# Expert slabs of a mixture-of-experts stage loaded as two transfers of 64 partitions instead of one of 128

## The reference

```python
def _moe(h, router, wg, wu, wd):
    logits = jnp.einsum('btd,de->bte', h, router).astype(jnp.float32)
    top_v, top_i = lax.top_k(logits, TOP_K)
    probs = jax.nn.softmax(top_v, axis=-1)
    ...
    for e in range(N_EXPERTS):
        y = y + combine[..., e:e + 1].astype(h.dtype) * _swiglu(h, wg[e], wu[e], wd[e])
```

## Time and profile before

| | us |
|---|---|
| Median of 3 runs (lowest to highest) | 1567.94 (1566.75 to 1570.85) |
| Profiled execution, its own time | 1572.46 |
| Its span (first to last instruction) | 1570.6 |
| PE busy in the span | 1526.9 (97%) |
| DVE, ACT, POOL busy | 631.3, 321.6, 56.3 |
| Queue 1 (SP's), share of 16 DMA engines over the span | 47.4% |

### The profile page before, as it was taken

The page is one execution under the profiler, slowest core; times in us unless marked ns, Lnnn a source line. Parts: engine busy times, 40 slices in busy tenths (PEclk is TensorE's granted clock), DMA queues, the critical chain, the costliest instruction groups (busy, mean ns, idle before and its releaser), DMA issues.

```text
span 1570.6 us, 39489 instructions
## 1 busy us (share of the span) xinstructions
PE 1526.9 (97%) x17595; PEld 1254.2 (80%) x17595; DVE 631.3 (40%) x1456; ACT 321.6 (20%) x759; POOL 56.3 (4%) x68
## 2 busy tenths in 40 slices
PE   9999999999999999999999999999999999999976
PEld 6877776887779999987887777877778797788765
DVE  5133346744145656562234267542241221122213
ACT  1432113222112222133321222221120000000001
POOL 1000010110000000000000000200010000000000
PEclk9999999999999999999999999999999999999998
DMA  8333435213544444346425252116779988989992
GB/s 338 108 107 115 168 116 138 88 30 85 207 143 159 142 155 161 108 169 249 155 101 207 93 137 94 44 64 210 309 297 340 335 304 332 342 297 335 354 401 98
DMA packets 64324, 299.71 MB, mean 191 GB/s; under 512 B 21839, under 2 KB 23567, under 8 KB 37663
## 3 DMA queue, kind: packets, MB, share of 16 engines
q1 hardware_dynamic: 50392, 268.10, 47.4%
q0 software_dynamic: 2944, 18.09, 3.1%
q10 hardware_dynamic: 10823, 11.05, 2.7%
HBM read 277.93 MB, written 19.28 MB: 189 GB/s over the span
## 4 chain that ended last, share of the span: by engine, by line
PE 93%; DVE 3%; issue 2%; DMA 1%; ACT 1%; SPq 0%; DVEq 0%; ACTq 0%
PE ps L1007 15%; PE ps L1593 15%; PE ps L1743 14%; PE ps L1468 11%; PE ps L1675 7%; PE ps L1475 6%; PE ps L1531 4%; PE ps L994 4%; PE ps L1324 2%; PE ps L1626 2%; DMA ring<-in_mix 1%; PE ps L1019 1%; PE ps L1300 1%; PE ps L1057 1%; PE ps L1372 0%
## 5 line engine op out<-in xcount | busy, mean ns | idle before, releaser
L1007 PE MATMUL ps<-xn,ring 128*128 128x288 f32 x928 | 238.1, 413 | 0.0
L1007 PEld LDWEIGHTS ps<-xn,ring 128*128 128x128 f32 x928 | 174.9, 192 | 50.8 <-issue 2.8
L1468 PE MATMUL ps<-xn,ring 128*128 128x288 f32 x768 | 203.0, 412 | 0.8 <-ACT gate L2074 0.4
L1468 PEld LDWEIGHTS ps<-xn,ring 128*128 128x128 f32 x768 | 142.1, 190 | 48.9 <-issue 11.7
L1593 PE MATMUL ps<-y_ml,arena 128*64 128x96 f32 (+5 forms) x3584 | 142.7, 242 | 17.1 <-issue 16.2
L1593 PEld LDWEIGHTS ps<-y_ml,arena 128*64 128x64 f32 x3584 | 139.1, 140 | 22.4 <-issue 22.3
L1743 PE MATMUL ps<-arena 128*128 128x144 f32 x1028 | 133.4, 285 | 0.9 <-DVE arena L2911 0.9
L1743 PEld LDWEIGHTS ps<-arena 128*128 128x128 f32 x1028 | 129.3, 189 | 1.0 <-issue 1.0
L1675 PE MATMUL ps<-arena,mixed 128*32 128x256 f32 x2024 | 112.2, 379 | 2.6 <-issue 2.6
L1675 PEld LDWEIGHTS ps<-arena,mixed 128*32 128x32 f32 x2024 | 65.9, 110 | 45.8 <-issue 4.0
L2859 DVE TENSOR_TENSOR mixed<-ps,mixed 128x96 f32<-128x96 f32 (+5 forms) x88 | 21.7, 247 | 193.8 <-PE ps L1593 193.6
(11 more groups left out here) (514 smaller groups left out, 1849.0 us busy)
## 6 DMA issues: line engine op xcount, KB each, us to landing
arena<-in_egu SPq DMA_DIRECT2D x56, 1024.0 KB, 6.0
ring<-in_mix SPq DMA_DIRECT2D x46, 1024.0 KB, 6.1
arena<-in_edown SPq DMA_DIRECT2D x40, 1024.0 KB, 6.5
ring<-in_mix SPq DMA_DIRECT2D x48, 768.0 KB, 4.3
ring<-in_egu SPq DMA_DIRECT2D x32, 1024.0 KB, 7.8
ring<-in_gu SPq DMA_DIRECT2D x14, 1024.0 KB, 4.9
arena<-in_gu SPq DMA_DIRECT2D x8, 1024.0 KB, 5.6
arena<-in_C POOLq DMA_DIRECT2D x2, 2048.0 KB, 8.3
```

The lines of the kernel that those rows point to most:

```text
L1007: last = mm(bank[:, 0:T], ring[:, s, w0:w0 + P], (xn if n else xgain)[:, k, :], start=(k == 0), stop=(k == KT - 1))
L1468: last = mm(ps[:, bank, 0:T], ring[:, s, P * k:P * k + P], xn[:, k, :], start=(k == 0), stop=(k == KT - 1))
```

## The change

Every expert slab is issued as two transfers: partitions 0 to 63 (`CH` = 64) and partitions 64 to 127, one behind the other on SP's queue, both adding 16 to the slab's semaphore. The three places that count on the semaphore now count 32 for a slab. The waits stand where they stood, and the bytes, the places and the order of the slabs are the same. Loads of the mixer's and the dense layer's weights stay single transfers.

```diff
+                def in_halves(k, width, src):
+                    for r in (slice(0, CH), slice(CH, P)):
+                        sp.dma_start(eslab(k)[r, 0:width], src[r]).then_inc(e_ld[k].sem, 16)
+
                 def first_expert(slabs):
                     for k in slabs:
-                        src = a["egu"][k] if k < FT else a["edown"][k - FT, :, 0:D * len(DOWN[k - FT])]
-                        sp.dma_start(eslab(k), src).then_inc(e_ld[k].sem, 16)
+                        width = SLOT if k < FT else D * len(DOWN[k - FT])
+                        in_halves(k, width, a["egu"][k] if k < FT else a["edown"][k - FT, :, 0:width])
...
                         if isinstance(p, int):
                             j = (k - IN_FLIGHT) % ETURNS
-                            sp.wait_ge(e_ld[j].sem, p * 16 + (16 if k >= IN_FLIGHT else 0) + expert_loads(j))
+                            sp.wait_ge(e_ld[j].sem, p * 32 + (32 if k >= IN_FLIGHT else 0) + expert_loads(j))
...
-                        sp.dma_start(eslab(k)[:, 0:width], src.rearrange("a p n -> p (a n)")).then_inc(e_ld[k].sem, 16)
+                        in_halves(k, width, src.rearrange("a p n -> p (a n)"))
...
             def loaded(p, k):
 
-                pe.wait_ge(e_ld[k].sem, p * 16 + 16 + expert_loads(k))
+                pe.wait_ge(e_ld[k].sem, p * 32 + 32 + expert_loads(k))
                 return eslab(k)
```

## The result

The changed kernel takes 1774.49 us (median of 4 runs, 1771.03 to 1777.28) against 1568.4 us before: 1.130 times as long, 95% interval 1.1287 to 1.132. The prediction said 1763. The profiled execution is the one of 1771.03 us, with a span of 1769.2.

A forecast was written before the change was run, and what follows sets the result against it. TensorE was taken to bound the kernel, the weight stream 10 us ahead. At 4.8 us a slab the stream takes over: span 1766, 195.8 above 1570.6; execution 1768; adjusted to the median, 1763 us, range 1640 to 1815.

The forecast's parts named there:

- What bounds it: Expert passes: TensorE sets the time, the weight stream leads by 10 us; over 0.1 us more a slab makes the stream the bound.
- Rate of a transfer to 64 partitions: Expert slabs in halves: DMA moves little more than half as fast, 4.8 us a slab, 218 GB/s, against 2.46 us.
- Before the passes: Last gate units: the fourth 768 KB load waits behind three halved slabs, +7.0 us, all on TensorE's path.
- The stream's end: Last slab lands at 1751.4 us; then 0.9 us of TensorE's down product and 14.1 us to the span's end.
- From the profile to the median: Whole kernel: 1768 us for the profiled execution, lowered because the earlier one lay 4.5 us above its median, to 1763.
- Issues, semaphores at nothing: SP's queue: 136 more issues of 0.43 us are covered by the other slab in flight; waiting for both halves adds 0.
- A cost for the second transfer: Rival, slab stream: each half costs its issue, 0.43 us a slab, +34 us after the lead, about 1602 us; chance 0.06.
- Drift: Rival, slab stream: paired DMA engines drift into opposite halves, half the effect, 3.6 us a slab, about 1606 us; chance 0.11.
- Not slower: Rival, slab stream: all 16 engines serve either half at full pace, 1568 us; chance 0.06 within 0.3%, 0.01 faster.
- TensorE's clock: Expert passes: a waiting TensorE may fall to 1.2 GHz of 2.4, adding up to 25 us, for an upper end of 1815.
- The signs: Passes: near 215 GB/s, share 0.95 or more, halves landing in 7 to 10 us, SP waits over 400, TensorE about 60% busy.

## Why the prediction was right

- **What bounds it.** Right. The lead of 10 us was used up and the stream became the bound. It was a thin cover: a loss of 0.2 us a slab by columns was enough to show as 20 us.
- **Rate of a transfer to 64 partitions.** The step that decided, and right in size: taken 4.8 us a slab and 218 GB/s, measured 222 GB/s in the fixed passes. Slab 0 of pass 7 landed at 1681.7 us and that of pass 1 at 1194.1 by the semaphore events, 487.6 us for 6 x 16.5 slabs, 4.93 us each with the token rows. The windows around the token-row fetches had carried it. That it comes from pairs of engines sharing a way into SBUF fits the runs of halves and quarters but is not shown, and 96 and 32 partitions are slower than its simplest form allows.
- **Before the passes.** +7.0 forecast for the fourth mixer load; it landed at 1088.47 + 19.3 = 1107.8 against 1100.5, +7.3, and TensorE started at 1108.04 against 1100.71. It waited 7.4 us over three of these loads, not 7 before the last one alone.
- **The stream's end.** Forecast 1751.4, measured 1715.13 + 38.1 = 1753.2. TensorE's down product ended 1.7 us later, at 1754.9 (forecast 0.9), and 14.3 us remained (14.1 before).
- **From the profile to the median.** Here 8 of the 11 us of the miss lie. The sum gave 1768 for the profiled execution and it took 1771.03, which is 3 us. I then took 4.5 us off because the profiled execution of the kernel before lay above its median; that of the changed kernel lies 3.5 below. The spread between executions is not a property that carries over.
- **Issues, semaphores at nothing.** Not quite for two transfers as such: with two slabs in flight they cost about 0.2 us a slab, the 20 us of the runs by columns and by even and odd partitions. For the columns it is the time of the packets and not SP's issue. No run shows how much of it is in the change, whose packets take 0.588 us for a reason of their own.
- **The rivals.** A cost for the second transfer exists, at some 20 of the 34 us, but not by the mechanism named, SP's issue behind a landing. Drift fits as a correction (222 instead of 213 GB/s) and not as half of the effect; that the rate rises with four in flight agrees with "an engine that runs ahead stops when SP has issued no further slab". Not slower is refuted by every run with contiguous halves.
- **TensorE's clock.** The granted clock is 0.92 in the fixed passes (1190 to 1490) and 0.77 in the loop pass, where TensorE stands idle before most slabs. TensorE is busy for 1585.7 us with the same 17595 records that took 1526.9 before. Those 59 us cost next to nothing: TensorE waited for the stream anyway, and the tail is 0.2 us longer. The 25 us of the upper end did not come.
- **The signs.** The rate, the share of 0.99 and the 8.3 us from issue to landing of a half (median of passes 1 to 7) came as written. Two did not. SP waited 355.8 us at the line that was 891, not over 400. TensorE is busy for 80% of 1190 to 1490 and for 73% of 1168 to 1755 (427.56 of 587 us), not for 60%: I had taken the busy time of before, at its clock. TensorE's idle time was put too high, and since the stream is the bound, the kernel's time does not show it.

## What to carry to other kernels

A load like these slabs (1 MB in rows of 8 KB) should spread its rows over the whole partition range in each transfer; if it has to be cut in two, cut it by columns or by even and odd partitions, and let three slabs be in flight (tried for the columns). A busy share of 1.0 does not say that DMA works at its rate: read the GB/s beside it, and look in the old trace for a small transfer of the shape that a change would introduce, since its window prices the change. A limit that is raised tests something only if it is still the one that binds. Where the stream has a lead of 10 us over 120 slabs, a tenth of a microsecond a slab is the whole of it.

## What the runs showed of the hardware

- Transfers to partitions 0-63 and 64-127 in turn run at 216 to 222 GB/s with two 1 MB slabs in flight, the same bytes in even and odd partitions at 309, in whole slabs at 330.
- A packet of 8 KB takes 0.309 us (median) in whole slabs and 0.588 in such halves.
- With such halves the rate rises with more in flight although the DMA share is 0.99 already: 222 GB/s at a limit of two slabs, 254 at four, 252 at eight, where SP waited mostly for TensorE to free a place.
- A transfer of 96 partitions followed by one of 32 is as slow as two halves (222 GB/s).
- What is queued behind such halves lands later: the fourth mixer load, which goes to all 128 partitions, came 7.3 us later behind three halved slabs.
